# Turning the tokens by a product with a scaled diagonal, in place of scaling them and transposing

## What is computed

```python
def rmsnorm(x, g):
    xf = x.astype(jnp.float32)
    y = xf * lax.rsqrt(jnp.mean(xf * xf, axis=-1, keepdims=True) + EPS)
    return (y * g.astype(jnp.float32)).astype(x.dtype)

def hybrid_layer(h, ...):
    xn = rmsnorm(h, norm_mix)
    z = xn @ w_in
    ...
```

## Time and profile before

| | |
|---|---|
| median of 3 runs | 1333.32 us (1331.97 to 1335.27) |
| the profiled execution's own time | 1332.77 us |
| its span in the profile | 1331.0 us, so 1.8 us lie around it |
| TensorE busy | 1314.0 us (99%) |
| VectorE busy | 840.4 us (63%) |
| ScalarE busy | 412.7 us (31%) |
| GpSimd busy | 524.3 us (39%) |

### The profile page before, as it was taken

One profiled execution on the slowest core, in us unless ns is written; L12 is line 12 of the kernel. 1 busy time (PEld: TensorE's weight loads), 2 busy tenths in 40 slices (PEclk: granted clock), 3 DMA queues, 4 the chain that ended last, 5 costly groups with the idle time before them and its releaser, 6 DMA issues.

```text
span 1331.0 us, 22484 instructions
## 1 busy us (share of the span) xinstructions
PE 1314.0 (99%) x8988; PEld 1282.5 (96%) x8988; DVE 840.4 (63%) x1414; ACT 412.7 (31%) x807; POOL 524.3 (39%) x544
## 2 busy tenths in 40 slices
PE   7999999999999999999999999999999999999997
PEld 6899999899999999999999999999999999999997
DVE  6566898436463665556666756756667567566866
ACT  7566652112221213232122222322222223222313
POOL 2322112111111211221367466574574755746811
PEclk9999999999999999999999999999999999999999
DMA  6223553633323323221111212112011121110213
GB/s 193 62 73 91 163 166 80 194 115 88 88 65 82 101 57 90 81 65 48 48 33 48 64 33 63 33 48 64 33 61 51 36 61 48 49 49 32 80 45 118
DMA packets 161947, 99.88 MB, mean 75 GB/s; under 512 B 19736, under 2 KB 156468, under 8 KB 161843
## 3 DMA queue, kind: packets, MB, share of 16 engines
q1 hardware_dynamic: 138866, 85.56, 21.9%
q10 hardware_dynamic: 22976, 12.88, 3.6%
HBM read 77.62 MB, written 20.80 MB: 74 GB/s over the span
## 4 chain that ended last, share of the span: by engine, by line
PE 93%; DVE 3%; ACT 2%; issue 1%; DMA 1%; SPq 0%; POOL 0%; DVEq 0%; ACTq 0%
PE banks L1401 10%; PE banks L1927 9%; PE banks L1403 9%; PE banks L1402 9%; PE banks L1929 9%; PE banks L1928 9%; PE banks L1946 7%; PE banks L1947 7%; PE banks L1945 7%; PE banks L1963 1%; PE banks L1964 1%; PE banks L1965 1%; PE banks L1621 1%; PE banks L1635 1%; PE banks L1857 1%
## 5 line engine op out<-in xcount | busy, mean ns | idle before, releaser
L1927 PE MATMUL banks<-hg_high,w_high 128*128 128x384 f32 (+1 forms) x768 | 249.5, 325 | 0.0
L1929 PE MATMUL banks<-hg_high,w_low 128*128 128x384 f32 (+1 forms) x768 | 247.6, 322 | 0.0
L1928 PE MATMUL banks<-hg_low,w_high 128*128 128x384 f32 (+1 forms) x768 | 247.3, 322 | 0.0
L2674 DVE TENSOR_TENSOR hT<-hT,banks 128x528 f32<-128x528 f32 x280 | 189.4, 701 | 84.0 <-PE banks L1947 76.0
L1401 PE MATMUL banks<-xn_high,w_high 128*128 128x384 f32 (+1 forms) x672 | 226.8, 337 | 0.6 <-DVE xn_low L2057 0.5
L1403 PE MATMUL banks<-xn_high,w_low 128*128 128x384 f32 (+1 forms) x672 | 218.1, 325 | 0.0
L1402 PE MATMUL banks<-xn_low,w_high 128*128 128x384 f32 (+1 forms) x672 | 218.0, 324 | 0.0
L821 POOL TENSOR_TENSOR w_low<-w_raw,w_high 128x1024 fp32r<-128x1024 f32 x31 | 77.0, 2483 | 243.7 <-ACT w_high L1015 243.7
L1927 PEld LDWEIGHTS banks<-hg_high,w_high 128*128 128x128 f32 x768 | 144.2, 188 | 1.9 <-POOL w_low L947 1.7
L1928 PEld LDWEIGHTS banks<-hg_low,w_high 128*128 128x128 f32 x768 | 144.3, 188 | 0.1
L1929 PEld LDWEIGHTS banks<-hg_high,w_low 128*128 128x128 f32 x768 | 144.2, 188 | 0.0
(11 more groups left out here) (333 smaller groups left out, 2783.6 us busy)
## 6 DMA issues: line engine op xcount, KB each, us to landing
w_raw<-in_w_up SPq DMA_DIRECT2D x32, 512.0 KB, 4.0
w_pair<-in_w_down SPq DMA_DIRECT2D x32, 512.0 KB, 3.4
w_raw<-in_w_in SPq DMA_DIRECT2D x28, 512.0 KB, 4.3
w_raw<-in_w_out SPq DMA_DIRECT2D x8, 512.0 KB, 4.1
x_slice<-in_x_prompt SPq DMA_DIRECT2D x8, 512.0 KB, 4.2
out<-y_tok SPq DMA_DIRECT2D x8, 512.0 KB, 2.7
v_kept_rows<-v_feat SPq DMA_DIRECT2D x4, 536.0 KB, 2.9
gate_kept_rows<-gate_row SPq DMA_DIRECT2D x4, 536.0 KB, 3.1
```

Source lines behind the costliest of these rows:

```text
L1927: pe.matmul(bank[:, 0:w], w_h[half][:, k, :], hg_h[:, k, c0:c0 + w], start=(k == 0), stop=False)
L1928: pe.matmul(bank[:, 0:w], w_h[half][:, k, :], hg_l[:, k, c0:c0 + w], start=False, stop=False)
L1929: ins = pe.matmul(bank[:, 0:w], w_l[half][:, k, :], hg_h[:, k, c0:c0 + w], start=False, stop=(k == KT - 1))
L2674: dve.tensor_tensor(hc, hc, both, ALU.add if sign > 0 else ALU.subtract).then_inc(acc_read_dve, 1)
```

## The change

For each tile VectorE now makes `x_root[t]`, the identity with its diagonal multiplied by the tile's `rx` (128 elements on each partition), and the tile itself stays as it came. TensorE multiplies each piece by that diagonal matrix in a plain product, which turns and scales at once. The two table products between the first tiles are gone, and those ahead of tile 0 stay (`IDLE_PRODUCTS`). ScalarE squares tile 3 behind step 7, ahead of tiles 4, 5 and 6, and VectorE takes tile 3's mean there.

```diff
+        x_root = [place(f"x_root{t}", [P, P], F32, RK + 16 * SLOT + 4 * P * t) for t in range(NT)]
...
-        SQUARE_AFTER = {7: (4, 5, 6), 8: (7,), 10: (8,)}
+        SQUARE_AFTER = {7: (3, 4, 5, 6), 8: (7,), 10: (8,)}
         AB_AFTER = 9
-        IDLE_PRODUCTS = (3, 1, 1)
+        IDLE_PRODUCTS = (3, 0, 0)
...
             act.activation(ab_w[:, :, 0:8], ab_raw[:, :, :], ACT.Copy).then_inc(ab_hi, 1)
-            square_x(3)
             act.wait_ge(rows_kept, 1)
...
                     if k == 0:
-                        pe.wait_ge(x_scaled, t + 1)
-                    ins = pe.transpose(ps[turn_bank(g, k)][:, o - c0:o - c0 + c], x_tile(t)[:, P * k:P * k + P],
-                                       eye[0:c, 0:c])
+                        pe.wait_ge(x_rooted, t + 1)
+                    ins = pe.matmul(ps[turn_bank(g, k)][:, o - c0:o - c0 + c], x_tile(t)[:, P * k:P * k + P],
+                                    x_root[t][0:c, 0:c], start=True, stop=True)
...
-                pe.wait_ge(x_scaled, t + 1)
+                pe.wait_ge(x_rooted, t + 1)
                 o, c = tile_cols(t)
                 for k in range(KT):
-                    ins = pe.transpose(ps[turn_bank(0, k)][:, o:o + c], x_tile(t)[:, P * k:P * k + P], eye[0:c, 0:c])
+                    ins = pe.matmul(ps[turn_bank(0, k)][:, o:o + c], x_tile(t)[:, P * k:P * k + P], x_root[t][0:c, 0:c],
+                                    start=True, stop=True)
...
-            def scale_x(t):
-
+            def root_x(t):
+
+                c = rows(t)
                 dve.wait_ge(x_pow, t + 1)
-                dve.tensor_scalar(x_tile(t), x_tile(t), rx[0:rows(t), t:t + 1], None, ALU.mult).then_inc(x_scaled, 1)
+                dve.tensor_scalar(x_root[t][0:c, 0:c], eye[0:c, 0:c], rx[0:c, t:t + 1], None, ALU.mult).then_inc(x_rooted, 1)
...
-            mean_x(3)
             for m in range(3 * KT):
...
                 if m == KT - 1:
-                    scale_x(3)
+                    mean_x(3)
+                    root_x(3)
```

More of the change, by code:

```diff
@@ L315, in build @@
         s_norm = sem("s_norm"); s_row = sem("s_row"); s_xin = [sem(f"s_xin{i}") for i in range(6)]; s_const = sem("s_const")
-        x_sq = sem("x_sq"); x_pow = sem("x_pow"); x_ms = sem("x_ms"); x_scaled = sem("x_scaled")
+        x_sq = sem("x_sq"); x_pow = sem("x_pow"); x_ms = sem("x_ms"); x_rooted = sem("x_rooted")
         x_turned = sem("x_turned"); x_high = sem("x_high"); x_low = sem("x_low")
@@ L2047, in _ @@
                     dve.tensor_copy(tn[:, :], ps[0][:, 0:16]).then_inc(rows_kept, 1)
-                scale_x(t)
+                root_x(t)
             dve.wait_ge(w_high, 1)
@@ L2060, in _ @@
                 if m == KT - 1:
-                    scale_x(3)
+                    mean_x(3)
+                    root_x(3)
                     mean_x(4)
                     mean_x(5)
-                    scale_x(4)
-                    scale_x(5)
+                    root_x(4)
+                    root_x(5)
                     mean_x(6)
                 if m == KT:
-                    scale_x(6)
+                    root_x(6)
                     mean_x(7)
                 if m == KT + 2:
-                    scale_x(7)
+                    root_x(7)
                     mean_x(8)
                 if m == KT + 3:
-                    scale_x(8)
+                    root_x(8)
             dve.wait_ge(rows_turned, 2)
```

## The result

The changed kernel takes 1339.14 us in the median of 6 runs (1338.26 to 1341.44), the kernel before 1333.17 us (1331.97 to 1335.27): a ratio of 1.0042, with a 95% interval of 1.0032 to 1.0053. It is slower by 0.42%, where 0.42% was forecast.

A forecast was written before the change was run, and what follows sets the result against it. TensorE was taken to bound the kernel, passing added work in the first 36 us on to the end; 2.1 + 1.2 + 2.25 = 5.55 us on 1332.77 us gave 1338.3 us, range 1335.6 to 1341.0 us.

The forecast's parts named there:

- The price of a piece: TensorE's turning: a product costs 0.2225 us at the high clock, 0.107 more than a transpose; 0.213 an instruction at the low.
- Term 1: Start, tiles 0 to 2: 48 slow TensorE instructions delay ScalarE's first `xn_high` to about 15.3 us, +2.1 us.
- Term 2: From the start to step 12: 25 products, partly hidden by TensorE's waits, with tile 5 otherwise unchanged, +1.2 us.
- Term 3: Steps 12 to 18: no wait left, so turning the pieces of steps 17 to 23 costs +2.25 us.
- The clock rises early: Rival, chance 0.22: TensorE's clock rises at about 11.3 us, the start costs only +0.4 us, 1336.6 us.
- The clock rises late: Rival, chance 0.12: TensorE's clock stays low through steps 0 to 7, the start costs 6.4 us, 1342.6 us.
- Not slower: Rival, chance 0.05: a product's two instructions lie so close that a piece costs what a transpose does, 1331.5 us.
- a dear product: Rival, chance 0.03: a product on TensorE costs clearly more than the trace's plain products show, 1342 us and above.

The follow-up runs named there:

- the first group alone: The change with diagonal products for tiles 0 to 2 only, tiles 3 to 8 scaled and transposed; ratio 1.0025 to the kernel before.
- the doubled pieces: The change with each piece of tiles 3 to 8 turned twice, the second time over the first; 1350.29 us, ratio 1.0127 to the kernel before.
- the later groups alone: The kernel before with diagonal products for tiles 3 to 8 only, keeping table products and tile 3's early square; ratio 1.0016 to the kernel before.
- the short filler: The change with three 128x384 products on a constant tile ahead of everything on TensorE; 1337.35 us, ratio 1.0020 to the kernel before.

## Why the prediction was right

**The price of a piece.** Right. At the high level it was taken from plain products of the same shape 270 us later, 0.2225 us, and steps from 12 on are 1.196 us apart for a predicted 1.18. At the low level no row had it, and the upper bound that I took, 0.213 us an instruction, was the value: 0.216 for tile 0, 0.22 over tiles 0 and 1.

**Term 1, the start, +2.1 us.** `xn_high` started 2.45 us later. Tile 0 began at 7.91 us, as worked out, but tile 2 at 15.05 and not at 14.7: besides the steps of 0.213 us, tile 1's first two instructions start 0.34 and 0.38 us behind the ones before them, which the sum did not have and no run explains. The clock rose only while tile 2's first instruction ran, and the first `xn_high` came at 15.62, not 15.3. In the profiles of the first group alone and of the doubled pieces, which start as the change does, the clock rose at about 14.2 and 14.4 us and `xn_high` began at 15.05 and 14.98. So part of the 2.45 us is this one execution's late rise. The start of the kernel before is no firmer: its `xn_high` stands behind the square of tile 3, whose transfer landed at 12.09 us and at 11.2 in the run of the later groups alone. From one profile each, term 1 is known to about a microsecond. That the scalings saved at this place gain nothing is shown: the diagonal was there 5 us too early. That the low clock makes the cost is shown by the run with the short filler, where the same instructions leave `xn_high` at 11.33 us.

**Term 2, to step 12, +1.2 us.** It was 31.58 - 27.48 - 2.45 = 1.65 us. The mis-sized part is tile 5. I had the additional square at 1.04 us and let it cancel against a shorter root and a shorter multiplication. These are rows of the chain, first of the kernel before (its square of tile 5, which the earlier trace rows leaves out), then of the changed kernel:

```profile
17.63 1.16 ACT square_out L1022 x2
```
```profile
20.10 1.16 ACT square_out L1023 x2
...
21.34 1.16 ACT square_out L1023 x2
```

Squares that follow each other start 1.24 us apart: between two of them ScalarE reads out the sum of the first. My 1.04 us was the chain's piece for a square that comes behind a high part; the square behind it already showed 1.16 in the kernel before. The root took 0.55 us instead of 1.00 and the diagonal 0.28 us (predicted 0.22) instead of 0.75, so tile 5 was 0.36 us later than the start alone made it (23.68 - 20.87 - 2.45). From there the sum of 25 products and four steps held: 7.90 us, predicted 7.8.

**Term 3, +2.25 us.** From step 12 to the mark it was (42.74 - 31.58) - (36.30 - 27.48) = 2.34 us.

**The sum.** 6.44 us at the mark in one execution, 5.6 us at equal mean clock, 0.42% by the medians, against 5.55 us. The mechanism was as forecast. The agreement to a tenth of a microsecond is luck: each of the three terms measured more than forecast in the profile, by 0.35, 0.45 and 0.09 us, and the medians have an interval of 1.4 us on either side.

**The rivals.** *The clock rises early* did not happen in the three profiles that begin as the change does (about 14.2, 14.4 and 15.2 us), and none of the change's six executions came near its 1336.6 us. But the run of the later groups alone had such a rise, at 11.9 us, behind the very instructions with which the kernel before had it after 14.38, so one profile could not have excluded it. *The clock rises late* happened in the run with the table products put back, at about 17.1 us; up to there it is hidden by ScalarE's and VectorE's pace, as worked out: from the first `xn_high` to the mark that run takes 44.03 - 16.90 = 27.13 us, and the change 27.12. *Not slower* and *a dear product* are excluded by the price of a piece, two instructions 0.11 us apart where a transpose is one.

## What to carry to other kernels

Folding a scaling into a transpose through a diagonal saves time on VectorE and doubles the transposes on TensorE; ask which of them the end waits for, and read the price from a product of that very shape elsewhere in the trace. Price a stretch at the clock that its own instructions show, not by the recorded one: the same 48 instructions took 9 us or 5.7 us here. A step moved out of the way of one chain lands in front of another: moving tile 3's square gained 1.46 us at the start and cost 1.2 us where it went, and together with the products it kept only the cost.

## What the runs showed of the hardware

The granted clock reads 1.00 in stretches where TensorE's instructions lie at the 1.2 GHz level (421 ns where the same form takes 275), up to about 15 us.

The moment of the rise differs by microseconds between single executions. With the same instructions ahead of it, it came between 14.4 and 14.7 us in the profile of the kernel before and at 11.9 us in that of the later groups alone. With the change's start it came at about 15.2, 14.2 and 14.4 us (the change, the first group alone, the doubled pieces). Each kernel was profiled once. So the other moments, 13.4 to 13.8 us with transposes and no table products, about 12.9 us with tile 0 by transposes and 17.1 us with the table products put back, can't be put down to the work that differs. What did bring it sooner in all four runs was products that start 4 us earlier: it had risen by the time tile 0 was turned, at 7.1 us in the earliest of them. No run here shows what sets the moment within that.

With TensorE busy throughout, the granted clock still falls in places, between 20 and 80 us and between 240 and 265 us (0.73 over 5 us in the change's profile), in some executions and not in others. None of the twelve profiles has a fall from 265 to 1310 us. The executions of the kernel before take 1.0, 2.0 and 2.5 us more at mean clocks of 0.997, 0.996 and 0.995 than at 0.998, and this is the larger part of their scatter.
